# Starting byte of the moving rows, by stage: 0 (or 64) before, four remainders of 128 after

## The chip, the cores and the metric

One core of one Trainium2 chip runs the whole program. The metric is the device time of that core in microseconds; the time before is 2819.22 us, the median of two runs (2818.82 and 2819.62).

## What is computed

Two transformer-like blocks over 512 tokens of width 1024, all in float32. The reference, cut to its frame:

```
for i in range(2):                                   # first block
    h = h + 0.5 * swiglu(rms_norm(h, ffn1_norm[i]), w_in, w_out)
    h = h + mixer(rms_norm(h, mix_norm[i]))          # recurrent, then spatial gating
    h = h + 0.5 * swiglu(rms_norm(h, ffn2_norm[i]), w_in, w_out)
h = rms_norm(h, final_norm)
h = h + merged @ w_out                               # attention, S5 and HGRN2 branches
h = h + cross_attention(rmsnorm(h), rmsnorm(mem), ...)
h = h + swiglu_2(rmsnorm(h), w_gate_up, w_down)
```

There are five feed-forward parts (numbered i = 0 to 4 below): up to 2 x 2816 columns, SiLU, and down to 1024.

## The kernel before

**Products in three passes.** Each float32 operand is split into a high and a low part (type F32R): ACT writes the high part (w_hi, xg_hi, h_hi), POOL or DVE the difference (w_lo, xg_lo, h_lo). A product of two tiles is three matmuls into the same bank: high by high (L460), high weights by low rows (L461), low weights by high rows (L462), in `three_passes`. Weights are the stationary operand, 128 x 128; the moving operand is one row of 512 tokens per partition, `hi` or `lo`.

**Stages.** x (x_res) holds the residual, [128, 8, 512]. At each norm, number q, xg_hi and xg_lo are written from x by the gains. The norms are q = 0, 2, 3, 5, 9 (the five feed-forward parts), 1 (recurrent mixer), 4 (spatial gating mixer), FINAL = 6 (input of the second block and its branches) and 8 (cross-attention). All nine use the same two buffers in turn.

**The up projection** (`pe_ffn`) runs its first units and its last body as plain three-pass products with 512-token rows: 192 such matmuls in each of parts 1 to 4, 288 in part 0. The rest goes in steps of seven block products of 12 matmuls each, with rows of 256 tokens (L716, L717, L718): three of them read halves of xg, four read xsum, a tile of four sums of blocks of x, high and low, [4, 2, 4, 256]. One step is 36 matmuls on xg and 48 on xsum; there are 16 steps in part 0 and 18 in each other part.

**The down projection** reads h_hi and h_lo, [22, 512] each, 528 matmuls in each part. h_raw lies where h_lo will be written.

**The mixers.** q = 1 has 16 units of 24 matmuls on xg rows, q = 4 has 8, q = 8 has 8, and q = FINAL has 48. In the value projections of q = 4 and FINAL and one branch (L547 to L549 and L2030 to L2032, 384 matmuls) xg is the stationary operand and the weights move.

**Addresses.** `place` gives every tile a fixed byte offset within the partition. x_res begins at a multiple of 2048 and the tiles up to `work` have sizes that are multiples of 2048, so xg_hi, xg_lo, w_hi, w_lo, h_hi and h_lo all begin at a multiple of 128, and so does each of their rows. mem_hi, mem_lo (the memory of the cross-attention), yh, sgy, y0, y1, merged and o begin at multiples of 1024 above `work`, too. One exception: xsum begins at `work + 64`, so each of its rows of 1024 bytes begins 64 bytes past a multiple of 128.

**Order.** SP loads weights into a ring of four units, ACT and POOL split them, PE multiplies, DVE and ACT take the banks. The order on every engine is written out by hand; semaphores alone hold it together.

Of the kernel before, what the change touches and what calls it, by code (L numbers as in the profile page):

```python
# [91 lines left out]
def build(nc, io):  # L92
# [51 lines left out]


    LINE = 2048
    cursor = [-(-nc.sbuf_base // 128) * 128]

    def place(name, shape, dt=F32, at=None):
# [12 lines left out]
    eps = place("eps", [P, 1])  # L162
    cursor[0] = -(-cursor[0] // LINE) * LINE
    x = place("x_res", [P, KD, T])
    xg_hi = place("xg_hi", [P, KD, T], F32R)
    xg_lo = place("xg_lo", [P, KD, T], F32R)
    w_stage = place("w_stage", [P, RING, UNIT])
    w_hi = place("w_hi", [P, RING, UNIT], F32R)
    w_lo = place("w_lo", [P, RING, UNIT], F32R)
# [6 lines left out]
    aux = cursor[0]  # L176
    cursor[0] += 8192
    work = cursor[0]
    h_hi = place("h_hi", [P, KF, T], F32R)
    h_lo = place("h_lo", [P, KF, T], F32R)  # L180
    par = place("par", [P, NPAR])
    ones = place("ones", [P, P])
    ident = place("ident", [P, P])
# [2 lines left out]
    KB = 1024  # L186


    h_raw = place("h_raw", [P, KF, T], at=work + KF * T * 4)
    xsum = place("xsum", [P, 4, 2, 4, HALF], F32R, at=work + 64)  # L190
    s1_w = place("s1_w", [P, 2, T], F32R, at=work + 33 * KB)
    s2_w = place("s2_w", [P, 2, T], F32R, at=work + 37 * KB)
    u_add0 = place("u_add0", [P, T], at=work + 41 * KB)
# [370 lines left out]
        return KD * (q - (q > FINAL))  # L564

    def act_norm_tile(act, q, gain, m, buf):
        act.activation(tile(xg_hi, m), tile(x, m), ACT.Copy, scale=col(*gain(m))).then_inc(xg_hi_ready, 1)
        act_norm_square(act, q, m, buf)

    def act_norm_square(act, q, m, buf):  # L570
# [3 lines left out]

    def dve_norm_tile(dve, q, gain, m, buf):
        dve.wait_ge(xg_hi_ready, m + (split_count(q) + 1))
        dve.scalar_tensor_tensor(tile(xg_lo, m), tile(x, m), col(*gain(m)), f32(tile(xg_hi, m)),
                                 ALU.mult, ALU.subtract).then_inc(xg_lo_ready, 1)
        dve_norm_add(dve, q, m, buf)
# [128 lines left out]

    def pe_ffn(pe, i, q):
        U, L = layers[f"up{i}"], layers[f"down{i}"]  # L710

        def product(out, w, v):
            (wh, wl), (xh, xl) = w, v
# [76 lines left out]
        each_body(pe, L.bodies, down)  # L790

    def pool_up(pool, U, i):

        def plain(b, u):
            if U.base == 0 and b == 0 and u == 1:
                pool.wait_ge(xg_lo_ready, KD)
            split_lo_unit(pool, U, b, u)

        def row(b, p, row):
            r = 2 * p + row  # L800
            cs = slice(row * T, 2 * T)
# [12 lines left out]

        def s3_low(n):
            pool.wait_ge(wsum_hi_ready, after_wsum_hi(i, "S3", n))
            pool.tensor_tensor(s3_w[:, 1], s3_f[:], f32(s3_w[:, 0]), ALU.subtract).then_inc(pool_lo_ready, 1)

        def scale_gate(j):

            pool.wait_ge(silu_done, j + (KF * i + 1))
            pool.tensor_tensor(gbuf[:], gbuf[:], rstd[:], ALU.mult).then_inc(silu_scaled, 1)

        def step(b, p, gate=True):
            n, b1, p1 = pair_at(b, p), b + p, 1 - p
            row(b1, p1, 0)
            if gate:
                scale_gate(n + 1)
            s3(n + 1, p1)
            row(b1, p1, 1)  # L830
            s3_low(n + 1)

        at = PLAIN_FIRST[i]
        n0 = pair_at(at, 0)
        for u in range(3):
            plain(0, u)
        if i == 0:
            plain(0, 3)
            for u in range(3):
                plain(1, u)  # L840
        pool.wait_ge(xsum_done, XSUMS * (i + 1))
        plain(at - 1, 3)
        s3(n0, 0)
        x_low(0)
        row(at, 0, 0)
        x_low(3)
        row(at, 0, 1)
        x_low(2)
        s3_low(n0)
        x_low(1)  # L850
        step(at, 0, gate=False)
        step(at, 1)
        with pool.Fori(at + 1, LAST - 1) as b:
            step(b, 0)
            step(b, 1)
        step(LAST - 1, 0)
        plain(LAST, 0)
        scale_gate(KF - 4)
        plain(LAST, 1)
        plain(LAST, 2)  # L860
        scale_gate(KF - 3)
        plain(LAST, 3)
# [5 lines left out]

    def act_x_high(act, i, t):
        act.wait_ge(xsum_done, XSUMS * i + XSUM_COUNT[t])  # L870
        act.activation(xsum[:, t, 0], xsum_f[:, 1 + t], ACT.Copy).then_inc(wsum_hi_ready, 1)

    def act_ffn_entry(act, i, gain):

# [24 lines left out]

    def act_ffn(act, i, gain):  # L900
        U, L = layers[f"up{i}"], layers[f"down{i}"]

        def row1(b, p):
            split_hi(act, U, b, 2 * p)
# [101 lines left out]

    def dve_ffn(dve, i, gain=None):
        U = layers[f"up{i}"]

        def wsum(name, b, n, p):  # L1010
            w11, w12, w22 = w_stage[:, 2 * p, 0:T], w_stage[:, 2 * p, T:2 * T], w_stage[:, 2 * p + 1, T:2 * T]
# [208 lines left out]
    def pe_rec(pe, q):  # L1220
# [12 lines left out]
        for s in range(2 * KD):  # L1233
            u = s % KD
            if s == KD + 4:
                pe.wait_ge(gates_sig, 2 * KD)
            project_unit(pe, R if s < KD else Y, u // 4, u % 4, xg_hi, xg_lo,
                         (xg_lo_ready, split_count(q)) if s == 0 else None, out=y_bank(u) if s >= KD else None)
            if s == 0:
                pe_norm_sum(pe, q)  # L1240
            if 0 <= s - GATES_AT < KD:
                gates(s - GATES_AT)
# [126 lines left out]
    def pe_sgu(pe, q):  # L1369
# [5 lines left out]
        def norms_read(pe):  # L1375
            pe.wait_ge(std_ready, q + 1)
            pe.wait_ge(col_std, 1)
        pe_project_tokens(pe, V, xg_hi, xg_lo, norm=norms, ready=(xg_lo_ready, split_count(q)), between=norms_read)

        def mix(h):  # L1380

# [6 lines left out]
                               start=True, stop=True)  # L1388
            mm.then_inc(mixed, 1)
        for u in range(KD):  # L1390
            project_unit(pe, U, u // 4, u % 4, xg_hi, xg_lo, free=V.rbase + u + 1 if u < 4 else None)
            if u == 2:
                pe.wait_ge(ws_ready, 1)
                mix(0)
                mix(1)
            if u >= 2:
                mix(u)
# [95 lines left out]
    def dve_final(dve, L):  # L1493
# [8 lines left out]
        def body(b):  # L1502
            for mm in range(4):
                m = b * 4 + mm
                dve.wait_ge(unit_used, b * L.per + (L.base + (mm + 1) * 3))
                dve.scalar_tensor_tensor(tile(x, m), bank[mm][:], 0.5, tile(x, m), ALU.mult, ALU.add).then_inc(taken, 1)
                dve.wait_ge(xg_hi_ready, m + (KD * FINAL + 1))
                dve.scalar_tensor_tensor(tile(xg_lo, m), tile(x, m), gain12[:, bass.ds(m, 1)], f32(tile(xg_hi, m)),
                                         ALU.mult, ALU.subtract).then_inc(xg_lo_ready, 1)
                dve.wait_ge(ss_added, m * 2 + added)  # L1510
# [10 lines left out]
    def act_final(act, L):  # L1521
        act.wait_ge(final_gain, 1)

        def result(b, i):
            if i % 3 == 2:
                m = b * 4 + i // 3
                act.wait_ge(taken, m + (L.rbase + 1))
                act.activation(tile(xg_hi, m), tile(x, m), ACT.Copy, scale=gain12[:, bass.ds(m, 1)]).then_inc(xg_hi_ready, 1)
                act.wait_ge(ss_added, m * 2 + ((KD + 1) * FINAL + 2))
                act.activation(sq[:, 0, :], tile(x, m), ACT.Square).then_inc(sq_ready, 1)  # L1530
                act.activation(sq[:, 1, :], tile(x, m), ACT.Square, scale=col("final_norm", m)).then_inc(sq_ready, 1)
# [82 lines left out]
    def pe_fox_unit(pe, kind, i):  # L1614
# [7 lines left out]
            pe.wait_ge(taken, L.rbase + i - 1)  # L1622
        else:
            pe.wait_ge(taken, L.rbase + i)
        for k in range(KD):
            mm = three_passes(pe, unit_bank(kind, i)[:], r, k, xg_hi[:, k, :], xg_lo[:, k, :], k == 0, k == KD - 1)
        mm.then_inc(unit_used, 1)
# [25 lines left out]

    def pe_mix(pe):
        V = layers["fox_v"]
        pe_project_tokens(pe, V, xg_hi, xg_lo, norm=pe_final_sums, ready=(xg_lo_ready, split_count(FINAL + 1)), norm_after=2)

        def pack_squares(p):
# [348 lines left out]
    def pe_s5(pe):  # L2007
        QFG, V, M = layers["hg_qfg"], layers["hg_v"], layers["merge01"]

        def first_half(u):  # L2010
# [7 lines left out]
                pe.wait_ge(w_lo_ready, V.base + u - 12 + 1)  # L2018
            half(u, 0)

        def half(u, part):

            if 12 <= u < 16:
# [258 lines left out]

    def pe_merge_gate(pe, b, p, i, ks=range(KD)):
        L, u, r, _ = triple(b, p)
        if ks[0] == 0:
            pe.wait_ge(w_lo_ready, L.base + u + i + 1)
            pe.wait_ge(taken, L.rbase + r + i + 1 - RING)
# [305 lines left out]

    def pe_cross(pe):
        Q, O = layers["xq"], layers["xo"]

        def q_half(u, part):
            if part == 0:
# [656 lines left out]
    def _(act):  # L3255
# [4 lines left out]
        split_hi(act, order[0], 0, 0)  # L3260
        for m in range(KD):
            act.wait_ge(x_in[m // 2], 32)
            act.activation(xg_hi[:, m, :], x[:, m, :], ACT.Copy, scale=col("ffn1_norm", m)).then_inc(xg_hi_ready, 1)
        split_hi(act, order[0], 0, 1)
        for m in range(KD):
            act_norm_square(act, 0, m, m % 2)
# [30 lines left out]
    def _(dve):  # L3297
        dve.wait_ge(par_in, 16)
        dve.memset(ss[:], 0.0).then_inc(ss_added, 1)
        for m in range(KD):  # L3300
            dve.wait_ge(x_in[m // 2], 32)
            dve.wait_ge(xg_hi_ready, m + 1)
            dve.scalar_tensor_tensor(xg_lo[:, m, :], x[:, m, :], col("ffn1_norm", m), f32(xg_hi[:, m, :]),
                                     ALU.mult, ALU.subtract).then_inc(xg_lo_ready, 1)
        for m in range(KD):
            dve_norm_add(dve, 0, m, m % 2)
# [170 lines left out]
```

## Time and profile before

| | |
|---|---|
| median of two runs | 2819.22 us |
| the profiled execution, its span | 2817.5 us |
| PE busy | 2790.9 us (99%), 16386 matmuls |
| weight loads (PEld) | 2391.3 us (85%) |
| DVE | 1657.6 us (59%) |
| POOL | 1571.1 us (56%) |
| ACT | 1346.4 us (48%) |
| matmuls on the chain that ended last | 94% of the span |
| DMA | 267.91 MB, mean 95 GB/s |

The time of a matmul in the profile includes its way through the array, so consecutive matmuls overlap in the listing: a 512-token matmul shows 389 ns but the next starts 0.22 or 0.23 us after it. What a matmul costs in a dense stretch is the distance from its start to the next start, and that is read from the timeline, or from a window divided by the matmuls that the program has in it.

### The profile page before, as it was taken

To read this page: it belongs to the slowest core of one execution; us is meant where nothing else is said; L and a number is where in the kernel's file an instruction comes from. 1 tells how busy PE (TensorE), PEld (TensorE's weight loads), DVE (VectorE), ACT (ScalarE), POOL (GpSimd) and SP (SyncE) were. 2 spreads that over 40 slices of the span, in tenths; PEclk is the share of its full clock that TensorE was granted. 3 is DMA by queue.
4 is the path that set the end of the run, shared out by engine and by line. 5 is a ranking of instruction groups with operands and counts; after the bars stand their busy time and mean duration, and the time that the engine had idled before them with its cause. 6 is when DMAs were issued, how large, how long until landed. Compare 5 with 4: busy or idle time off the path is not lost.

```text
span 2817.5 us, 45558 instructions
## 1 busy us (share of the span) xinstructions
PE 2790.9 (99%) x16386; PEld 2391.3 (85%) x16386; DVE 1657.6 (59%) x2703; ACT 1346.4 (48%) x2076; POOL 1571.1 (56%) x872
## 2 busy tenths in 40 slices
PE   8999999999999999999999999999999999999999
PEld 6998877899889998888999886665688888799987
DVE  6777147677616774135777416579788464477730
ACT  5554257555425554243555334557444444455531
POOL 6775445677547774444777443158633373367743
PEclk9999999999999999999999999999999999999999
DMA  3234322232332233332223332112222342123332
GB/s 136 105 104 115 103 82 82 91 104 104 111 99 90 104 109 105 100 106 89 91 104 120 101 94 77 53 53 66 71 89 70 103 149 75 53 103 107 109 98 77
DMA packets 80685, 267.91 MB, mean 95 GB/s; under 512 B 11168, under 2 KB 13216, under 8 KB 80560
## 3 DMA queue, kind: packets, MB, share of 16 engines
q1 hardware_dynamic: 77904, 262.01, 28.4%
q10 hardware_dynamic: 2656, 4.26, 0.5%
q8 instruction: 74, 1.21, 0.2%
q14 instruction: 51, 0.42, 0.0%
HBM read 263.09 MB, written 2.10 MB: 94 GB/s over the span
## 4 chain that ended last, share of the span: by engine, by line
PE 94%; DVE 3%; ACT 1%; issue 1%; DMA 0%; POOL 0%; ACTq 0%; SPq 0%; DVEq 0%
PE bank L460 17%; PE bank L462 17%; PE bank L461 17%; PE bank L716 10%; PE bank L718 10%; PE bank L717 10%; PE bank L547 1%; PE bank L548 1%; PE bank L549 1%; PE bank L1635 1%; PE bank L2047 1%; PE bank L2915 1%; PE bank L2647 0%; PE bank L2056 0%; PE bank L2627 0%
## 5 line engine op out<-in xcount | busy, mean ns | idle before, releaser
L448 POOL TENSOR_TENSOR w_lo<-w_stage,w_hi 128x1024 fp32r<-128x1024 f32 (+1 forms) x228 | 535.2, 2353 | 714.0 <-ACT w_hi L424 713.5
L424 ACT ACTIVATE w_hi<-w_stage 128x1024 fp32r<-128x1024 f32 (+1 forms) x412 | 421.0, 1027 | 367.2 <-PE bank L462 303.5
L803 POOL TENSOR_TENSOR w_lo<-w_stage,w_hi 128x1024 fp32r<-128x1024 f32 (+1 forms) x176 | 327.3, 1859 | 202.1 <-ACT w_hi L424 202.1
L460 PE MATMUL bank<-xg_hi,w_hi 128*128 128x512 f32 x976 | 396.2, 406 | 5.0 <-DVE h_raw L1063 3.8
L461 PE MATMUL bank<-xg_lo,w_hi 128*128 128x512 f32 x976 | 381.2, 391 | 0.0
L462 PE MATMUL bank<-xg_hi,w_lo 128*128 128x512 f32 x976 | 381.2, 391 | 0.0
L455 POOL TENSOR_TENSOR w_lo<-w_stage,w_hi 128x1024 fp32r<-128x1024 f32 (+1 forms) x96 | 234.9, 2453 | 261.7 <-ACT w_hi L424 217.3
L460 PE MATMUL bank<-h_hi,w_hi 128*128 128x512 f32 x880 | 342.3, 389 | 0.0
L461 PE MATMUL bank<-h_lo,w_hi 128*128 128x512 f32 x880 | 342.3, 389 | 0.0
L462 PE MATMUL bank<-h_hi,w_lo 128*128 128x512 f32 x880 | 342.3, 389 | 0.0
L718 PE MATMUL bank<-xg_hi,w_lo 128*128 128x256 f32 x1056 | 299.2, 283 | 0.0
L716 PE MATMUL bank<-xg_hi,w_hi 128*128 128x256 f32 x1056 | 298.9, 283 | 0.0
L717 PE MATMUL bank<-xg_lo,w_hi 128*128 128x256 f32 x1056 | 298.8, 283 | 0.0
L716 PE MATMUL bank<-xsum,s_w 128*128 128x256 f32 x1056 | 296.1, 280 | 0.0
L718 PE MATMUL bank<-xsum,s_w 128*128 128x256 f32 x1056 | 294.6, 279 | 0.0
L717 PE MATMUL bank<-xsum,s_w 128*128 128x256 f32 x1056 | 294.6, 279 | 0.0
L1136 DVE SCALAR_TENSOR_TENSOR x_res<-bank,x_res 128x512 f32 x64 | 44.0, 687 | 400.9 <-PE bank L462 400.9
L460 PEld LDWEIGHTS bank<-xg_hi,w_hi 128*128 128x128 f32 x976 | 183.6, 188 | 72.5 <-issue 34.5
L1028 DVE TENSOR_TENSOR s_w<-bank,s_w 128x512 fp32r<-128x512 f32 x176 | 121.7, 691 | 190.4 <-ACT s_w L933 190.4
L461 PEld LDWEIGHTS bank<-xg_lo,w_hi 128*128 128x128 f32 x976 | 183.9, 188 | 40.5 <-issue 4.8
L462 PEld LDWEIGHTS bank<-xg_hi,w_lo 128*128 128x128 f32 x976 | 183.6, 188 | 39.7
L716 PEld LDWEIGHTS bank<-xg_hi,w_hi 128*128 128x128 f32 x1056 | 202.4, 192 | 0.2
(530 smaller groups left out, 6599.0 us busy)
## 6 DMA issues: line engine op xcount, KB each, us to landing
w_stage<-w_up SPq DMA_DIRECT2D x220, 512.0 KB, 4.2
w_stage<-w_down SPq DMA_DIRECT2D x80, 512.0 KB, 3.5
w_stage<-merge SPq DMA_DIRECT2D x36, 512.0 KB, 3.4
w_stage<-w_down SPq DMA_DIRECT2D x40, 384.0 KB, 3.2
w_stage<-hg_qfg SPq DMA_DIRECT2D x12, 512.0 KB, 3.4
w_stage<-rec_r SPq DMA_DIRECT2D x8, 512.0 KB, 3.5
w_stage<-rec_y SPq DMA_DIRECT2D x8, 512.0 KB, 3.4
w_stage<-rec_out SPq DMA_DIRECT2D x8, 512.0 KB, 3.4
```

What stands on the lines that cost most here:

```text
L424: act.activation(w_hi[:, r, 0:w], w_stage[:, r, 0:w], ACT.Copy).then_inc(w_hi_ready, 1)
L448: pool.tensor_tensor(w_lo[:, r, 0:w], w_stage[:, r, 0:w], f32(w_hi[:, r, 0:w]), ALU.subtract).then_inc(w_lo_ready, 1)
L455: pool.tensor_tensor(w_lo[:, r, 0:w], w_stage[:, r, 0:w], f32(w_hi[:, r, 0:w]), ALU.subtract).then_inc(w_lo_ready, 1)
L460: pe.matmul(out, w_hi[:, r, c], hi, start=start, stop=False)
L461: pe.matmul(out, w_hi[:, r, c], lo, start=False, stop=False)
L462: return pe.matmul(out, w_lo[:, r, c], hi, start=False, stop=stop)
L716: pe.matmul(out, wh[:, c], xh[:, k, :], start=k == 0, stop=False)
L717: pe.matmul(out, wh[:, c], xl[:, k, :], start=False, stop=False)
L718: mm = pe.matmul(out, wl[:, c], xh[:, k, :], start=False, stop=k == 3)
L803: pool.tensor_tensor(w_lo[:, r, cs], w_stage[:, r, cs], f32(w_hi[:, r, cs]), ALU.subtract).then_inc(w_lo_ready, 1)
L1028: dve.tensor_tensor(lo, src[:], f32(hi), ALU.subtract).then_inc(wsum_lo_ready, 1)
L1136: dve.scalar_tensor_tensor(tile(x, m), bank[mm % 4][:], scale, tile(x, m), ALU.mult, ALU.add).then_inc(taken, 1)
```

## The change

Nothing is computed differently and nothing is reordered: every engine has the same instructions in the same order, with other addresses. The buffer pair of xg is replaced by nine views into a region that is larger by 2 x 2048 bytes, one pair for each norm; h_hi, h_lo, h_raw and xsum get one view per feed-forward part, in a work region that is also larger by 2 x 2048 bytes. Each view begins at a remainder of 0, 32, 64 or 96 bytes by 128, and since rows are 1024 or 2048 bytes long each row of it does. The DMA scratch that the program reserves at the front of the on-chip memory is set to 1024 bytes, which frees the space.

```
+    XG_REMAINDER = {0: (64, 64), 1: (0, 96), 2: (32, 32), 3: (96, 96), 4: (64, 0), 5: (0, 64), FINAL: (64, 64), 8: (96, 32),
+                    9: (0, 32)}
+    XSUM_REMAINDER = (32, 96, 0, 64, 64)
+    H_REMAINDER = ((64, 64), (32, 32), (96, 96), (0, 64), (32, 96))
...
-    xg_hi = place("xg_hi", [P, KD, T], F32R)
-    xg_lo = place("xg_lo", [P, KD, T], F32R)
+    XG_BASE = cursor[0]
+    xg_of = {q: (place(f"xg_hi{q}", [P, KD, T], F32R, at=XG_BASE + high),
+                 place(f"xg_lo{q}", [P, KD, T], F32R, at=XG_BASE + KD * T * 4 + LINE + low)) for q, (high, low) in XG_REMAINDER.items()}
+    cursor[0] += 2 * (KD * T * 4 + LINE)
...
-    h_hi = place("h_hi", [P, KF, T], F32R)
-    h_lo = place("h_lo", [P, KF, T], F32R)
+    h_of = [(place(f"h_hi{i}", [P, KF, T], F32R, at=work + high),
+             place(f"h_lo{i}", [P, KF, T], F32R, at=work + KF * T * 4 + LINE + low)) for i, (high, low) in enumerate(H_REMAINDER)]
+    cursor[0] += 2 * (KF * T * 4 + LINE)
...
-    h_raw = place("h_raw", [P, KF, T], at=work + KF * T * 4)
-    xsum = place("xsum", [P, 4, 2, 4, HALF], F32R, at=work + 64)
+    h_raw_of = [place(f"h_raw{i}", [P, KF, T], at=work + KF * T * 4 + LINE + low) for i, (_, low) in enumerate(H_REMAINDER)]
+    xsum_of = [place(f"xsum{i}", [P, 4, 2, 4, HALF], F32R, at=work + off) for i, off in enumerate(XSUM_REMAINDER)]
...
     def pe_ffn(pe, i, q):
         U, L = layers[f"up{i}"], layers[f"down{i}"]
+        xg_hi, xg_lo = xg_of[q]
+        h_hi, h_lo = h_of[i]
+        xsum = xsum_of[i]
...
-    nc = bacc.Bacc("TRN2", target_bir_lowering=False, num_devices=1)
+    nc = bacc.Bacc("TRN2", target_bir_lowering=False, num_devices=1, dynamic_dma_scratch_size=1024)
```

The other lines of the diff replace the names xg_hi, xg_lo, h_hi, h_lo, h_raw and xsum by the view of the stage at hand.

By what the moving rows of a matmul have (high, low), the matmuls that the change touches are:

| remainders | 512-token rows | 256-token rows |
|---|---|---|
| 64 and 64 (part 0: xg, h; FINAL: xg) | 288 + 528 + 1152 = 1968 | 576 |
| 32 and 32, 96 and 96, 32 and 96, 96 and 32 (parts 1, 2: xg, h; part 4: h; q = 8: xg) | 720 + 720 + 528 + 192 = 2160 | 1296 |
| 0 with 64, 64 with 0 (part 3: xg, h; q = 4: xg) | 720 + 192 = 912 | 648 |
| 0 with 32, 0 with 96 (part 4: xg; q = 1: xg) | 192 + 384 = 576 | 648 |
| xsum 64 to 32 or 96 (parts 0, 1) | | 768 + 864 = 1632 |
| xsum 64 to 0 (part 2) | | 864 |
| xsum unchanged at 64 (parts 3, 4) | | 1728 |

## Rows read from the trace of the kernel before

**Rows 1.** The page: span, busy times, granted clock, and the chain's shares.
```profile
span 2817.5 us, 45558 instructions
...
PE 2790.9 (99%) x16386; PEld 2391.3 (85%) x16386; DVE 1657.6 (59%) x2703; ACT 1346.4 (48%) x2076; POOL 1571.1 (56%) x872
...
PEclk9999999999999999999999999999999999999999
...
PE 94%; DVE 3%; ACT 1%; issue 1%; DMA 0%; POOL 0%; ACTq 0%; SPq 0%; DVEq 0%
```

**Rows 2.** Waits of PE, longest first: whom it waited for, total, times, longest.
```profile
PE bank L486 <- ACT xg_hi L3263: 8.2, 1, 8.2
PE bank L460 <- DVE h_raw L1063: 3.8, 1, 3.8
```

**Rows 3.** One down projection, then up: window, its length, PE busy (records), clock, DMA.
```profile
1080.20:1199.90 119.70, 119.70 (x530) 1.00 0.33 99
1362.10:1541.70 179.60, 179.60 (x1513) 1.00 0.32 112
```

**Rows 4.** Timeline, PE, 512-token rows: start, time, operation (first and last of 47).
```profile
868.19 0.39 PE L461 MATMUL bank<-xg_lo,w_hi 128*128 128x512 f32 x1
...
878.85 0.28 PE L716 MATMUL bank<-xg_hi,w_hi 128*128 128x256 f32 x1
```

**Rows 5.** Timeline, PE: 256-token rows of xg, first and last of 31.
```profile
947.79 0.28 PE L718 MATMUL bank<-xg_hi,w_lo 128*128 128x256 f32 x1
...
951.51 0.28 PE L716 MATMUL bank<-xsum,s_w 128*128 128x256 f32 x1
```

**Rows 6.** Timeline, PE: 256-token rows of mem, eleven starts.
```profile
2254.80 0.28 PE L462 MATMUL bank<-mem_hi,w_lo 128*128 128x256 f32 x1
...
2256.00 0.28 PE L460 MATMUL bank<-mem_hi,w_hi 128*128 128x256 f32 x1
```

**Rows 7.** Timeline, PE: the 48 xsum matmuls of a step in steady running.
```profile
941.53 0.28 PE L716 MATMUL bank<-xsum,s_w 128*128 128x256 f32 x1
941.65 0.28 PE L717 MATMUL bank<-xsum,s_w 128*128 128x256 f32 x1
...
947.19 0.29 PE L716 MATMUL bank<-xg_hi,w_hi 128*128 128x256 f32 x1
947.32 0.28 PE L717 MATMUL bank<-xg_lo,w_hi 128*128 128x256 f32 x1
947.43 0.29 PE L718 MATMUL bank<-xg_hi,w_lo 128*128 128x256 f32 x1
```

**Rows 8.** Timeline, PE: the xsum matmuls behind a hesitation at 891.78.
```profile
891.58 0.28 PE L718 MATMUL bank<-xg_hi,w_lo 128*128 128x256 f32 x1
891.78 0.35 PE L716 MATMUL bank<-xsum,s_w 128*128 128x256 f32 x1
891.97 0.28 PE L717 MATMUL bank<-xsum,s_w 128*128 128x256 f32 x1
...
897.29 0.28 PE L716 MATMUL bank<-xg_hi,w_hi 128*128 128x256 f32 x1
```

**Rows 9.** Timeline, PE: 512-token rows after a hesitation, in the recurrent mixer.
```profile
475.81 0.40 PE L461 MATMUL bank<-yh_lo,w_hi 128*128 128x512 f32 x1
476.05 0.39 PE L462 MATMUL bank<-yh_hi,w_lo 128*128 128x512 f32 x1
...
477.19 0.39 PE L461 MATMUL bank<-yh_lo,w_hi 128*128 128x512 f32 x1
```

**Rows 10.** Groups of weight loads, 940 to 960 us: busy, mean ns.
```profile
L716 PEld LDWEIGHTS bank<-xg_hi,w_hi 128*128 128x128 f32 x25 | 4.8, 192 | 0.0
L716 PEld LDWEIGHTS bank<-xsum,s_w 128*128 128x128 f32 x24 | 4.5, 188 | 0.0
```

**Rows 11.** POOL's waits in the up projections, and the page's DMA queues.
```profile
POOL w_lo L803 <- ACT w_hi L424: 202.1, 79, 4.8
...
q1 hardware_dynamic: 77904, 262.01, 28.4%
q10 hardware_dynamic: 2656, 4.26, 0.5%
```

More of the change, by code:

```diff
@@ L566, in act_norm_tile @@
     def act_norm_tile(act, q, gain, m, buf):
-        act.activation(tile(xg_hi, m), tile(x, m), ACT.Copy, scale=col(*gain(m))).then_inc(xg_hi_ready, 1)
+        act.activation(tile(xg_of[q][0], m), tile(x, m), ACT.Copy, scale=col(*gain(m))).then_inc(xg_hi_ready, 1)
         act_norm_square(act, q, m, buf)
@@ L710, in pe_ffn @@
         U, L = layers[f"up{i}"], layers[f"down{i}"]
+        xg_hi, xg_lo = xg_of[q]
+        h_hi, h_lo = h_of[i]
+        xsum = xsum_of[i]
         def product(out, w, v):
@@ L792, in pool_up @@
     def pool_up(pool, U, i):
+        xsum = xsum_of[i]
         def plain(b, u):
@@ L870, in act_x_high @@
         act.wait_ge(xsum_done, XSUMS * i + XSUM_COUNT[t])
-        act.activation(xsum[:, t, 0], xsum_f[:, 1 + t], ACT.Copy).then_inc(wsum_hi_ready, 1)
+        act.activation(xsum_of[i][:, t, 0], xsum_f[:, 1 + t], ACT.Copy).then_inc(wsum_hi_ready, 1)
     def act_ffn_entry(act, i, gain):
@@ L901, in act_ffn @@
         U, L = layers[f"up{i}"], layers[f"down{i}"]
+        h_hi, h_raw = h_of[i][0], h_raw_of[i]
         def row1(b, p):
@@ L1008, in dve_ffn @@
         U = layers[f"up{i}"]
+        (h_hi, h_lo), h_raw = h_of[i], h_raw_of[i]
         def wsum(name, b, n, p):
@@ L1236, in pe_rec @@
                 pe.wait_ge(gates_sig, 2 * KD)
-            project_unit(pe, R if s < KD else Y, u // 4, u % 4, xg_hi, xg_lo,
+            project_unit(pe, R if s < KD else Y, u // 4, u % 4, *xg_of[q],
                          (xg_lo_ready, split_count(q)) if s == 0 else None, out=y_bank(u) if s >= KD else None)
@@ L1377, in norms_read @@
             pe.wait_ge(col_std, 1)
-        pe_project_tokens(pe, V, xg_hi, xg_lo, norm=norms, ready=(xg_lo_ready, split_count(q)), between=norms_read)
+        pe_project_tokens(pe, V, *xg_of[q], norm=norms, ready=(xg_lo_ready, split_count(q)), between=norms_read)
         def mix(h):
@@ L1390, in pe_sgu @@
         for u in range(KD):
-            project_unit(pe, U, u // 4, u % 4, xg_hi, xg_lo, free=V.rbase + u + 1 if u < 4 else None)
+            project_unit(pe, U, u // 4, u % 4, *xg_of[q], free=V.rbase + u + 1 if u < 4 else None)
             if u == 2:
@@ L1507, in body @@
                 dve.wait_ge(xg_hi_ready, m + (KD * FINAL + 1))
+                xg_hi, xg_lo = xg_of[FINAL]
                 dve.scalar_tensor_tensor(tile(xg_lo, m), tile(x, m), gain12[:, bass.ds(m, 1)], f32(tile(xg_hi, m)),
@@ L1527, in result @@
                 act.wait_ge(taken, m + (L.rbase + 1))
-                act.activation(tile(xg_hi, m), tile(x, m), ACT.Copy, scale=gain12[:, bass.ds(m, 1)]).then_inc(xg_hi_ready, 1)
+                act.activation(tile(xg_of[FINAL][0], m), tile(x, m), ACT.Copy, scale=gain12[:, bass.ds(m, 1)]).then_inc(xg_hi_ready, 1)
                 act.wait_ge(ss_added, m * 2 + ((KD + 1) * FINAL + 2))
@@ L1624, in pe_fox_unit @@
             pe.wait_ge(taken, L.rbase + i)
+        xg_hi, xg_lo = xg_of[FINAL]
         for k in range(KD):
@@ L1655, in pe_mix @@
         V = layers["fox_v"]
+        xg_hi, xg_lo = xg_of[FINAL]
         pe_project_tokens(pe, V, xg_hi, xg_lo, norm=pe_final_sums, ready=(xg_lo_ready, split_count(FINAL + 1)), norm_after=2)
@@ L2019, in first_half @@
             half(u, 0)
+        xg_hi, xg_lo = xg_of[FINAL]
         def half(u, part):
@@ L2284, in pe_merge_gate @@
         L, u, r, _ = triple(b, p)
+        xg_hi, xg_lo = xg_of[FINAL]
         if ks[0] == 0:
@@ L2595, in pe_cross @@
         Q, O = layers["xq"], layers["xo"]
+        xg_hi, xg_lo = xg_of[8]
         def q_half(u, part):
@@ L3262, in _ @@
             act.wait_ge(x_in[m // 2], 32)
-            act.activation(xg_hi[:, m, :], x[:, m, :], ACT.Copy, scale=col("ffn1_norm", m)).then_inc(xg_hi_ready, 1)
+            act.activation(xg_of[0][0][:, m, :], x[:, m, :], ACT.Copy, scale=col("ffn1_norm", m)).then_inc(xg_hi_ready, 1)
         split_hi(act, order[0], 0, 1)
@@ L3302, in _ @@
             dve.wait_ge(xg_hi_ready, m + 1)
-            dve.scalar_tensor_tensor(xg_lo[:, m, :], x[:, m, :], col("ffn1_norm", m), f32(xg_hi[:, m, :]),
+            dve.scalar_tensor_tensor(xg_of[0][1][:, m, :], x[:, m, :], col("ffn1_norm", m), f32(xg_of[0][0][:, m, :]),
                                      ALU.mult, ALU.subtract).then_inc(xg_lo_ready, 1)
```

## Prediction

> **What bounds the kernel now.** I read the page first. PE is busy for 2790.9 of 2817.5 us, its clock is at full rate in all 40 slices (the higher of its two levels, 2.4 GHz), and matmuls make 94% of the chain that ended last [rows 1]. Then the waits of PE: the longest is 8.2 us at the very start, the next 3.8 us, so there is no stall of any size to win [rows 2]. What is left is the rate of the stream of matmuls itself, and for that busy time says nothing; I go to the distance between starts.
>
> At 2.4 GHz and one column a cycle, a row of 512 tokens takes 213.3 ns and one of 256 takes 106.7 ns. The starts are further apart:
>
> - 512-token rows at remainder 0: a down projection has 528 matmuls in 119.7 us, 226.7 ns each [rows 3]; in the timeline 47 of them take 10.66 us, 226.8 ns each [rows 4]. That is 13.3 ns over the columns.
> - 256-token rows of xg at remainder 0: 31 take 3.72 us, 120.0 ns [rows 5]. Again 13.3 ns over.
> - 256-token rows of mem, also at remainder 0, but 1024 bytes apart as the rows of xsum are: ten take 1.20 us, 120.0 ns [rows 6].
> - 256-token rows of xsum at remainder 64: 48 take 5.66 us, 117.9 ns [rows 7], 11.2 ns over.
> - the same rows in the one step that follows a hesitation of PE: from 891.97 to 897.29 there are 47 matmuls in 5.32 us, 113.2 ns each [rows 8], 6.5 ns over.
>
> So every matmul pays a fixed 6.5 to 13.3 ns at its edge, whatever its length, and the sum over the span is large: 5616 + 3168 matmuls at 13.3 ns and 4224 at 11.2 are 164 us. The edge cost differs between remainder 0 and remainder 64, and at 64 it has two steady values, one of which is entered by a pause and left again at the next xg row. The rows of mem are what makes me put the difference to the remainder and not to the distance between rows or to the tile.
>
> **The change part by part.** No instruction is added, removed or moved; each term is (matmuls touched) x (change of distance). The counts are in the table of the change.
>
> *64 with 64: 1968 + 576 = 2544 matmuls.* The nearest rows are those of xsum. Between 120.0 and 117.9 the gain is 2.1 ns; between 120.0 and 113.2 it is 6.8. In these stages no row at 0 comes between to break the better rhythm, but I can't see how it is entered at 512 tokens, and in part 0 xsum, at 32, comes between. I take the middle, 4.45 ns: 2544 x 4.45 = 11.3 us gained (5.3 to 17.3).
>
> *32 and 96 with each other or themselves: 2160 + 1296 = 3456 matmuls.* No moving row of the trace has such a remainder. It could be as good as the best row seen (-6.8 ns), and a row that begins in mid-unit could cost the same again. For the far side the nearest row is that of 512-token matmuls which have just lost their rhythm: 475.81 to 477.19 is six in 1.38 us, 230 ns, 3.3 over the settled 226.7, and the first of them takes 0.24 us, up to 13 over [rows 9]; I put the far bound between, at +6.8. Halfway is nothing: 0 us, with -23.5 and +23.5 as bounds.
>
> *0 with 64 or 64 with 0: 912 + 648 = 1560 matmuls.* A third or two thirds of the rows are at 64, and the passes alternate. Alternation itself has a price in the trace: the entry from xg to xsum takes 0.12 us, and after the return to xg the starts are at 947.19, 947.32, 947.43, one longer and one shorter [rows 7]; it evens out. I take a third of 4.45: 1560 x 1.5 = 2.3 us gained (0 to 10.6).
>
> *0 with 32 or 96: 576 + 648 = 1224.* As the 32 and 96 case, a third of the rows: 0 us, bounds -2.8 and +2.8; and if mixed pairs behave as their worse member, +8.3.
>
> *xsum.* At 0 (864 matmuls) it should run as xg and mem do, 120.0 for 117.9: 1.8 us lost. At 32 and 96 (1632 matmuls) I take the same 120.0, as I took nothing against 0 for the others: 3.4 us lost, bounds 113.2 (7.7 gained) and 126.8 (14.5 lost). Unchanged at 64 (1728): 0, but up to 8.1 us gained if the better rhythm now holds.
>
> *xg as the stationary operand, 384 matmuls.* The weight loads beside xg rows at 0 take 192 ns and those beside xsum at 64 take 188 [rows 10]; they run beside the matmul before them, and PE waits for none. 0 us, with 384 x 6.8 = 2.6 us either way.
>
> *Other engines.* ACT, DVE and POOL write and read the same sizes at other starts. They have room: POOL in the up projections waits 202.1 us for ACT [rows 11], and PE waits for none of them [rows 2]. If one were slower by a tenth it would still be covered; without this cover each split of a unit would be on the path. A faster PE by 3 to 6% in a stage leaves the same room. The queues that carry data are hardware queues [rows 11], so the smaller scratch costs nothing.
>
> Sum: -11.3 + 0 - 2.3 + 0 + 1.8 + 3.4 = -8.4 us. The profiled execution would go from 2817.5 to 2809.1 us; the median of the runs lies 1.7 above the span, so I forecast **2811 us**.
>
> The Trainium skill, TensorE: Matmul & The Clock Gate, section "Back-to-back issue gap", gives a spacing of columns over 2.4 GHz plus about 2.5 ns. By that page rows of 512 would stand at 215.8 ns and rows of 256 at 109.2 ns, wherever they begin. The trace has 226.7 and 120.0 [rows 3, 5] and so disagrees: there is an excess in this stream that the page does not know.
>
> **The rivals.**
>
> *The remainder does nothing* (chance 0.17). The difference between xg and xsum would come from the tile's place or from what runs beside it. For it: within a tile at 64 the distance has two values without any change of address [rows 7, 8], so the remainder does not set it alone. Against it: mem at 0 behaves as xg [rows 5, 6]. Time: 2819 us, within 3. The Trainium skill, Advanced Engine Details and Errata, section "SBUF Cachelines", has lines of 16 bytes; by that page all four remainders begin on a line and nothing would change. No row here tells lines of 16 bytes from others.
>
> *Only the coincidence with the weights is dear* (chance 0.25). Weight rows begin at 0, and a load runs beside each matmul; it takes 192 ns beside rows at 0 and 188 beside rows at 64 [rows 10]. If any other start than 0 avoids the collision, then the 32 and 96 rows gain the same 4.45 ns, and mixed pairs half. 6000 x 4.45 = 26.7, 2784 x 2.2 = 6.1, less 1.8 for xsum at 0: 31 us faster, 2788 us. Against it: at 512 tokens the loads show 188 ns and yet 13.3 ns are lost. The Trainium skill, TensorE: Matmul & The Clock Gate, section "Step-by-step: what each phase is for", says that weights and moving rows come through two independent read ports; by that page this rival falls.
>
> *A row that begins within a unit of 64 bytes needs one fetch more* (chance 0.16, slower than before). The step between the edge costs seen, 13.3 and 6.5 ns, is the time of 16 columns, 64 bytes. Rows at 32 or 96 would cover one such unit more: 3456 x 6.8 = 23.5, a third of 1224 x 6.8 = 2.8, xsum at 32 and 96 at 126.8: 1632 x 8.9 = 14.5, xsum at 0: 1.8; less 11.3 and 2.3. That is +29 us, 2848 us. It decides the sign: break-even is where an off-unit row costs 1.5 ns more than a row at 0 (5496 such rows, counted as above, against the 8.4 us of the forecast).
>
> *The better rhythm takes over* (chance 0.07). All rows but those at 0 at 6.8 ns less, xsum at 113.2: 5616 + 3168 matmuls at 6.8 is 59.7, xsum 3360 x 4.7 = 15.8, less 1.8: about 74 us faster, 2745 us.
>
> *Off-unit rows lose far more than an edge* (chance 0.04): read at half rate, 3456 + 1632 matmuls would each take 100 ns or more on top, over 500 us. The trace shows no such row, hence the small chance is not zero.
>
> The forecast itself, only 64 helping and 32 and 96 being about as 0, has 0.31.
>
> **How the numbers follow.** The forecast alone spans 2800 to 2820. The range for 8 in 10 takes in the coincidence, nothing, and the extra fetch, and leaves out the last two and the tails: 2776 to 2850 us. Two per cent is about what a measurement of this kernel can tell from no change: 2762.8 and 2875.6 us. Faster by more than that needs most of the better rhythm: 0.07, and a little of the coincidence at its full 6.8 ns, 0.02. Slower by more needs the half-rate case or twice the extra fetch: 0.05. The rest, 0.86, is within.
>
> **What would show each step.** In the timeline: h of part 0 and xg of FINAL (64, 64) at 222 ns a matmul, the down projection of part 0 near 117.5 us instead of 119.7; parts 1 and 2 (32 and 96) at 119.7 still; xsum of part 2 at 120.0. The coincidence rival shows parts 1, 2 and 4 as short as part 0; the extra fetch shows them at 233 ns, 123 us; the rival of no effect leaves all at 119.7. I am wrong altogether if PE gets waits that it did not have, or if equal remainders give different distances in different parts without a pause between.

## The result and the profile after

The changed kernel takes 2842.74 us (median of two runs, 2842.48 and 2843.01) against 2819.22 us. The ratio is 1.0077 with an interval of 1.0053 to 1.0102: 23.5 us slower. The time is inside the range of the prediction and on the other side of its forecast, 2811.

The page of the kernel after, the rows that answer to [rows 1]:

```profile
span 2840.7 us, 45558 instructions
...
PE 2811.4 (99%) x16386; PEld 2387.6 (84%) x16386; DVE 1660.8 (58%) x2703; ACT 1346.0 (47%) x2076; POOL 1573.2 (55%) x872
...
PEclk9999999999999999999999999999999999999999
...
PE 94%; DVE 3%; ACT 1%; issue 1%; DMA 0%; POOL 0%; ACTq 0%; SPq 0%; DVEq 0%
```

The span is 23.2 us longer with the same instructions, the same clock and the same chain. The waits of PE, to hold against [rows 2]:

```profile
PE bank L493 <- ACT xg_hi L3284: 8.5, 1, 8.5
PE bank L467 <- DVE h_raw L1077: 6.5, 1, 6.5
```

They are 3.0 us longer together. Both lie in the first 42 us; in the traces of the other kernels below the second is between 2.7 and 4.3 us, so its 6.5 is at least in part a matter of the single execution. About 20 us went into the stream of matmuls. The five down projections of the kernel after, in windows that begin with their first matmul and end with the one behind their last, or, for the fifth, which has none behind it, with the start of its last (columns: window, its length, PE busy with records, clock, DMA):

```profile
244.70:365.60 120.90, 120.90 (x530) 1.00 0.33 98
740.20:863.40 123.20, 123.20 (x529) 1.00 0.31 96
1090.40:1213.60 123.20, 123.20 (x530) 1.00 0.32 96
1578.60:1701.10 122.50, 122.50 (x530) 1.00 0.30 88
2714.60:2837.00 122.40, 122.40 (x528) 1.00 0.28 86
```

Before, each of them took 119.7 us [rows 3], the fifth 119.5 to the start of its last matmul. From the start of the first matmul to the start of the last (527 distances, which is finer than a window read to 0.1 us) one distance is 228.9 ns for h at (64,64), 233.3 for (32,32) and for (96,96), 232.0 for (0,64) and 232.2 for (32,96), against 226.7. The five add up to 612.2 us against 598.3: 13.9 us of the 23.

The 256-token rows went the other way. Timeline of PE in the kernel after, the 36 matmuls on xg of a step in part 0, first and the one behind the last:

```profile
122.92 0.28 PE L727 MATMUL bank<-xg_hi,w_hi 128*128 128x256 f32 x1
...
127.16 0.28 PE L727 MATMUL bank<-xsum,s_w 128*128 128x256 f32 x1
```

4.24 us for 36, 117.8 ns each, where they had 120.0 [rows 5].

I summed the distances from start to start in both traces by stage and row length. The shares of the 23 us (a span of values goes over the stages, each with its own remainders):

| rows | before to after, ns a matmul | sum, us |
|---|---|---|
| h, 512 tokens | 226.7 to 228.9 ... 233.3 | +13.9 |
| xg, 512 tokens (waits in between included) | about 227 to 229 ... 233 | +10.3 |
| weights of 512 moving, xg stationary | 227 to 233 | +2.0 |
| xg, 256 tokens | 120.1 to 117.6 ... 120.0 | -5.5 |
| xsum, 256 tokens | 117.8 to 116.8 (32), 119.8 (96), 119.8 (0) | +2.0 |

The third line was not in my sum as a cost. Timeline of PE in the kernel after, 17 distances where the weights move and xg at (64,0) is loaded:

```profile
1226.02 0.40 PE L555 MATMUL bank<-w_hi,xg_lo 128*128 128x512 f32 x1
...
1229.99 0.39 PE L554 MATMUL bank<-w_hi,xg_hi 128*128 128x512 f32 x1
```

3.97 us for 17, 233.5 ns, though the moving rows begin at 0 as before.

The settled distances are not spread evenly. A product of two tiles is three matmuls, and three of them take 680.0 ns at 226.7, 686.7 at 228.9 and 700.0 at 233.3; kernels below have 693.3, at 231.1. That is a step of 6.67 ns each time. At 256 tokens three matmuls take 360.0 ns at 120.0, 353.3 at 117.8 and 340.0 at 113.3: one such step down from the first to the second, and two more to the third. Values between, as 232.0 and 232.2, are averages over longer patterns. The traces show the steps, not their cause.

### The profile page after: what moved, and what is told of

The parts are those of the page before. It is cut to its first block, busy times and chain, and to the rows that moved or that the text cites. A ratio compares the mean times of both kernels' runs of the same rounds, so it can differ in the third digit from the quotient of the medians.

```text
span 2840.7 us, 45558 instructions
## 1 busy us (share of the span) xinstructions
PE 2811.4 (99%) x16386; PEld 2387.6 (84%) x16386; DVE 1660.8 (58%) x2703; ACT 1346.0 (47%) x2076; POOL 1573.2 (55%) x872
## 4 chain that ended last, share of the span: by engine, by line
PE 94%; DVE 3%; ACT 1%; issue 1%; DMA 0%; POOL 0%; ACTq 0%; SPq 0%; DVEq 0%
PE bank L467 18%; PE bank L469 17%; PE bank L468 17%; PE bank L729 10%; PE bank L727 10%; PE bank L728 10%; PE bank L556 1%; PE bank L555 1%; PE bank L554 1%; PE bank L1651 1%; PE bank L2066 1%; PE bank L2936 1%; PE bank L2668 0%; PE bank L2075 0%; PE bank L2648 0%
## 5 line engine op out<-in xcount | busy, mean ns | idle before, releaser
L467 PEld LDWEIGHTS bank<-xg_hi,w_hi 128*128 128x128 f32 x976 | 183.7, 188 | 78.2 <-issue 37.2
L728 PEld LDWEIGHTS bank<-xsum,s_w 128*128 128x128 f32 x1056 | 199.6, 189 | 0.0
```

Of the source, the lines that this page charges most:

```text
L467: pe.matmul(out, w_hi[:, r, c], hi, start=start, stop=False)
L728: pe.matmul(out, wh[:, c], xl[:, k, :], start=False, stop=False)
```

## The experiments

All kernels are the changed one with other numbers in its three tables; in four of them the weight tiles are moved too. Distances are read from each kernel's own trace. Ratios are against the kernel before on the same chip.

**1. Layout or remainders, and whose.** Four kernels. The first has every remainder as before in the changed layout:

```
-    XG_REMAINDER = {0: (64, 64), 1: (0, 96), 2: (32, 32), 3: (96, 96), 4: (64, 0), 5: (0, 64), FINAL: (64, 64), 8: (96, 32),
-                    9: (0, 32)}
-    XSUM_REMAINDER = (32, 96, 0, 64, 64)
-    H_REMAINDER = ((64, 64), (32, 32), (96, 96), (0, 64), (32, 96))
+    XG_REMAINDER = {0: (0, 0), 1: (0, 0), 2: (0, 0), 3: (0, 0), 4: (0, 0), 5: (0, 0), FINAL: (0, 0), 8: (0, 0), 9: (0, 0)}
+    XSUM_REMAINDER = (64, 64, 64, 64, 64)
+    H_REMAINDER = ((0, 0), (0, 0), (0, 0), (0, 0), (0, 0))
```

> The changed kernel with every remainder as before: xg and h at 0, xsum at 64, in the changed layout (regions larger by 4 x 2048 bytes, w and work tiles moved, scratch 1024). The theory that the remainders cost the time: 2819 us, down projections 119.7 us each, as in the kernel before. The rival that the layout or the scratch costs it: about 2843 us.

Measured: 2819.27 us, ratio 0.9993 (0.9983 to 1.0003). Larger regions, moved weights and the smaller scratch cost nothing; the remainders are the cause. In its trace the five down projections stand at 226.7 ns again.

The second keeps only the H_REMAINDER of the change, the third only its XG_REMAINDER, the fourth only its XSUM_REMAINDER.

> Only h has the new remainders; xg at 0, xsum at 64. If each matmul pays by its own row's remainder, the five down projections keep the lengths of the changed kernel, 120.9, 123.2, 123.2, 122.5 and 122.4 us against 119.7, which is +13.9 us in sum: 2833 us. If the loss comes from what surrounds them (the rhythm brought in from the up projection, xg), they return towards 119.7 and the time is under 2825.

Measured: 2835.27 us, ratio 1.0047 (1.003 to 1.0064), 14.8 us over the kernel before in the same comparison (2820.48). Its down projections, in order:

```profile
246.50:367.40 120.90, 120.90 (x530) 1.00 0.33 98
740.00:863.20 123.20, 123.20 (x529) 1.00 0.31 96
...
1574.50:1697.00 122.50, 122.50 (x529) 1.00 0.29 88
2712.50:2834.90 122.40, 122.40 (x529) 1.00 0.29 86
```

These are the lengths of the changed kernel to 0.1 us, whatever the up projection ahead of them has, and so is the third, left out here, at 123.3 us. For 512-token rows the cost is local to the rows.

> Only xg has the new remainders; h at 0, xsum at 64. Summing the distances between starts over xg rows in the traces of before and after gives +7 us: 2826 us, the 512-token rows slower (227 to 229 to 233 ns), the 256-token rows faster (120 to about 118). If rows influence each other, xsum at 64 beside xg at 64 (part 0) takes up the better rhythm, 113.3 ns, and the time is lower by up to 3.5 us.

Measured: 2823.01 us, ratio 1.0007 (0.9997 to 1.0016). The 512-token rows were slower by as much as in the changed kernel. Less was lost than expected because part 1, with xg at (32,32) and xsum at 64, ran its xsum rows at 114.4 ns instead of 117.9, 3 us. Part 0, with both at 64, did not: 117.6 ns. The guess of the expectation on where the better rhythm would appear was wrong.

> Only xsum has the new remainders (32, 96, 0, 64, 64); xg and h at 0. By the distances in the two traces the xsum rows give -0.8, +1.6, +1.8, -0.2, -0.3 us: +2 us, 2821 us. If the distance of xsum is set by its own remainder alone, part 2 (now at 0, as xg) stands at 120.0 ns and parts 3 and 4 at 117.9 exactly as before.

Measured: 2823.64 us, ratio 1.0011 (1.0002 to 1.0021). xsum at 96 and at 0 stands at 120.1 and 120.0 ns, 1.8 and 2.0 us; at 32, with xg at 0, it stands at 117.9, not at the 116.8 that it has beside xg at 64. So for 256-token rows the neighbours count. The three parts of the change make 14.8 + 2.5 + 3.2 = 20.5 us of the 23.5. The intervals of these ratios are 5 to 10 us wide, so the times alone would not show what is missing; the traces do: part 1 gained 3.0 us on xsum only while xsum stayed at 64.

**2. The unit.** The weights stay at 0 and h gets pairs that the change did not have.

```
+    H_REMAINDER = ((64, 0), (0, 32), (32, 0), (128, 128), (64, 32))
```

> xg at 0, xsum at 64; h of the five parts at (64,0), (0,32), (32,0), (128,128), (64,32). The period is 128 if part 3 stands at 226.7 ns, as (0,0). If a row pays by its own remainder alone, a pair is the weighted mean of its two values (0: 226.7, 64: 229.0, 32: 233.3; high rows count twice): 228.2, 228.9, 231.1, 226.7, 230.4 ns. If the change from one remainder to the other also costs, as (0,64) with 232.0 in the changed kernel suggests, the mixed pairs are well above that, up to 233.

Measured, ns a matmul: 233.3, 231.7, 233.3, 233.3, 231.1. (128,128) was meant as a repeat of (0,0):

```profile
1574.40:1697.60 123.20, 123.20 (x530) 1.00 0.29 88
```

123.2 us instead of 119.7. "Remainder by 128" is the wrong description. And a pair need not be the mean of its members: (64,0) costs more than either (64,64) or (0,0).

**3. Against what.** The weights w_hi and w_lo are moved, to 64 and then to 32 above a multiple of 128.

```
-    w_hi = place("w_hi", [P, RING, UNIT], F32R)
-    w_lo = place("w_lo", [P, RING, UNIT], F32R)
+    w_hi = place("w_hi", [P, RING, UNIT], F32R, at=cursor[0] + 64)
+    w_lo = place("w_lo", [P, RING, UNIT], F32R, at=cursor[0] + RING * UNIT * 4 + 128 + 64)
+    cursor[0] += 2 * RING * UNIT * 4 + LINE
+    H_REMAINDER = ((0, 0), (64, 64), (32, 32), (96, 96), (64, 0))
```

> The weights w_hi and w_lo begin at 64 in all stages; h of the parts at (0,0), (64,64), (32,32), (96,96), (64,0). If only the moving row's own remainder counts, the first four down projections stand at 226.7, 229.0, 233.3, 233.3 ns a matmul as with the weights at 0. If the distance between the remainders of weights and rows counts, 0 and 64 change places: 229.0, 226.7, 233.3, 233.3. If the weights add their own share, as the stationary xg at 64 did in the changed kernel (233.3 ns), all are dearer, the first at 233.3.

> The weights begin at 32; h at (0,0), (64,64), (32,32), (96,96), (32,96). Only the row's own remainder: 226.7, 229.0, 233.3, 233.3, 232.2 ns. The distance between both: (32,32) stands at 226.7, (96,96) at 229.0, (0,0) and (64,64) at 233.3. Own share of the weights: every part is above its value with the weights at 0, by up to 6.7 ns.

Measured, one execution each, weights at 64: 231.8, 231.1, 233.3, 233.3, 231.1 ns; weights at 32: 231.1, 233.3, 231.1, 233.3, 231.1. All three readings fail as they were put. But the weights' place does count: with not one byte of h moved, the first part went from 119.7 to 122.4 us. What spoils these two runs is that w_lo lies another 128 bytes further on than w_hi, which I had thought to be no shift at all.

The whole time of the kernel with the weights at 64, 2835.05 us, hides its best part. Timeline of PE, the 36 matmuls on xg of a step in part 2 and the row behind them:

```profile
947.17 0.29 PE L727 MATMUL bank<-xg_hi,w_hi 128*128 128x256 f32 x1
...
951.29 0.28 PE L727 MATMUL bank<-xsum,s_w 128*128 128x256 f32 x1
```

4.12 us for 36 is 114.4 ns, where the kernel before has 120.0, and all five parts have it. Summed over the trace the 256-token rows of xg gained 18.0 us and those of xsum 2.6, with no moving row of the up projections shifted by a byte. The down projections and the other 512-token rows took it back. So at 256 tokens the place of the weights counts as well. The five placements of h beside these weights all cost 231.1 ns or more; no other was tried.

So once more, cleanly, with starts counted from a multiple of 2048. First with the weights at 0 and h at larger steps:

```
+    H_REMAINDER = ((256, 256), (512, 512), (1024, 1024), (192, 192), (0, 128))
```

> Weights at 0, xg at 0, xsum at 64; h of the five parts at (256,256), (512,512), (1024,1024), (192,192), (0,128). The pair (128,128) stood at 233.3 ns, not at the 226.7 of (0,0), so 128 bytes is not the period of the effect. If the period is 256, the first three parts stand at 226.7 ns and (192,192) at 229.0 (as 64) or 233.3 (as 32 and 96). If it is 512, 1024 or 2048, the first, the first two or all three are above 226.7. If any start but a multiple of 2048 is dear, all five stand at 229 to 233.

```profile
243.90:363.60 119.70, 119.70 (x529) 1.00 0.33 99
736.20:855.90 119.70, 119.70 (x530) 1.00 0.32 99
1079.90:1199.60 119.70, 119.70 (x529) 1.00 0.33 99
1563.40:1686.60 123.20, 123.20 (x529) 1.00 0.29 88
2697.60:2818.20 120.60, 120.60 (x528) 1.00 0.29 87
```

256, 512 and 1024 bytes are as good as 0; 192 costs the full 233.3 ns. The fifth, (0,128), stands at 228.9 ns, which for once is the mean of its members, with the high rows counted twice. Of the periods that these starts can tell apart it is 256 bytes.

Then with both weight tiles at 64, and with both at 128:

```
-    w_hi = place("w_hi", [P, RING, UNIT], F32R)
-    w_lo = place("w_lo", [P, RING, UNIT], F32R)
+    w_hi = place("w_hi", [P, RING, UNIT], F32R, at=cursor[0] + 64)
+    w_lo = place("w_lo", [P, RING, UNIT], F32R, at=cursor[0] + RING * UNIT * 4 + LINE + 64)
+    cursor[0] += 2 * (RING * UNIT * 4 + LINE)
+    H_REMAINDER = ((0, 0), (64, 64), (128, 128), (256, 256), (32, 32))
```

> Both w_hi and w_lo exactly 64 bytes above a multiple of 2048 (in the run with the weights at 64, w_lo lay at 192 by 256, which counts if 128 is not the period); h at (0,0), (64,64), (128,128), (256,256), (32,32). If the distance between rows and weights sets the cost, (64,64) stands at 226.7 ns and (0,0) above. If absolute starts set it, (64,64) stands at 229.0 or above, and no part reaches 226.7.

```profile
243.60:366.80 123.20, 123.20 (x530) 1.00 0.32 96
739.80:859.50 119.70, 119.70 (x530) 1.00 0.33 99
1081.60:1202.50 120.90, 120.90 (x530) 1.00 0.32 98
1567.10:1690.30 123.20, 123.20 (x530) 1.00 0.29 88
2708.70:2831.60 122.90, 122.90 (x528) 1.00 0.28 86
```

Rows at 64 are now the cheapest, 119.7 us, and rows at 0 are dear, 123.2.

> Weights exactly 128 above a multiple of 2048; h at (0,0), (128,128), (64,64), (256,256), (192,192). Distance between rows and weights: (128,128) at 226.7 ns, (192,192) at 229.0 as (64,64) with the weights at 0, (0,0) and (256,256) above. Absolute starts: (128,128) at 233.3 again.

```profile
242.40:365.60 123.20, 123.20 (x530) 1.00 0.32 96
737.30:857.00 119.70, 119.70 (x529) 1.00 0.32 99
1078.40:1201.60 123.20, 123.20 (x529) 1.00 0.31 96
1565.90:1689.00 123.10, 123.10 (x529) 1.00 0.29 88
2705.50:2826.10 120.60, 120.60 (x528) 1.00 0.29 87
```

With d = (start of the moving row - start of the weights) by 256 bytes, every down projection of the kernels that have w_hi and w_lo at the same place, and h_hi and h_lo too, falls into one table:

| d | weights at 0 | weights at 64 | weights at 128 |
|---|---|---|---|
| 0 | 226.7 (h at 0, 256, 512, 1024) | 226.7 (64) | 226.7 (128) |
| 64 | 228.9 (64) | 228.9 (128) | 228.9 (192) |
| 32, 96, 224 | 233.3 (32; 96) | 233.3 (32) | |
| 128 | 233.3 (128) | | 233.3 (0; 256) |
| 192 | 233.3 (192) | 233.3 (0; 256) | 233.3 (64) |

The stationary xg fits in as well. With both parts of xg at 64 and the moving weights at 0 (the changed kernel, FINAL) d is 192, and 72 matmuls stood at 233.4 ns; with xg at 0 and the moving weights at 64 d is 64, and the same 72 stood at 229.0. The (64,0) above, 233.5, is a mixed pair.

The other 512-token rows agree less exactly. With the weights at 128 and rows at 0 the distances in the mixers and up projections run from about 232 to 233.3 ns, and xg at 160 with the weights at 0 stood at 234.2. Only multiples of 32 bytes were tried. What it is in the chip that pays by this distance no run shows.

**4. The 256-token rows.** Tables of xg and xsum with h and the mixers at 0. A scan by part:

```
+    XG_REMAINDER = {0: (32, 32), 1: (0, 0), 2: (32, 0), 3: (32, 64), 4: (0, 0), 5: (64, 32), FINAL: (0, 0), 8: (0, 0), 9: (32, 96)}
+    XSUM_REMAINDER = (64, 64, 64, 64, 64)
```

> h at 0, mixers at 0, xsum at 64 in all parts; xg of the five parts at (32,32), (32,0), (32,64), (64,32), (32,96). With xg at (32,32) beside xsum at 64 the run of xg alone had 114.4 ns on xsum and 117.1 on xg in part 1. If that goes by the remainders, part 0 shows the same 114.4 and 117.1, and a matmul's distance is set by its neighbours' remainders as well as its own; if it was an accident of that part's entry, part 0 stays at 117.9. Time between 2812 and 2822 us.

Measured: 2812.6 us in its one timed run (before: 2819.98). Part 0 stayed at 117.6 ns on xsum although (32,32) with 64 had given part 1 114.4: the same starts, two rhythms. Part 1, now at (32,0), had 113.8; the others 117.8. This is close to the sign by which the prediction was to be wrong altogether, equal remainders with different distances in different parts, though here across two kernels.

The pair (32,0) in all five parts:

> h and mixers at 0, xsum at 64, xg of all five parts at (32,0). Part 1 had 113.8 ns on xsum, 118.0 on xg of 256 and 231.1 on xg of 512 with it, 4.2 us less than before. If the remainders give this, five parts give 21 us: 2798 us. If it was part 1's own entry, the other parts have 117.9 on xsum and the time is 2808 to 2813 us.

Measured: 2799.91 us, ratio 0.9925 (0.9908 to 0.9941): 0.75% faster than the kernel before, the best of all. The better rhythm holds in every part, at 113.8 to 114.1 ns over all steps, and is worth 16.7 us by the distances; the 256-token rows of xg gained 6.9, its 512-token rows lost about 4. Timeline of PE, the 48 xsum matmuls of a step in part 2 and the row behind them:

```profile
952.35 0.28 PE L726 MATMUL bank<-xsum,s_w 128*128 128x256 f32 x1
...
957.79 0.28 PE L726 MATMUL bank<-xg_hi,w_hi 128*128 128x256 f32 x1
```

5.44 us for 48 is 113.3 ns; the same 48 took 5.66 before [rows 7].

Then the guess that d = 192 is best at this length, since rows of mem at 0 beside weights at 64 ran so. Timeline of PE in the kernel with both weight tiles at 64, 20 distances:

```profile
2268.02 0.28 PE L468 MATMUL bank<-mem_lo,w_hi 128*128 128x256 f32 x1
...
2270.29 0.30 PE L467 MATMUL bank<-mem_hi,w_hi 128*128 128x256 f32 x1
```

2.27 us for 20 is 113.5 ns. Against the guess stood, in the same kernel, that the 256-token rows of xg, also at d = 192, had 117.8.

> Weights, h and mixers at 0 by 256; xg of the feed-forward parts and xsum at 192. With the weights at 64 and rows at 0 (a distance of 192 by 256) the undisturbed 256-token rows stood at 113.5 ns. If the distance alone sets it, all 256-token rows stand at 113.3: xg 648 x 6.7 = 4.3 us and xsum 864 x 4.6 = 4.0 us gained in a part, less 192 x 6.6 = 1.3 us for its 512-token rows (233.3, as every row at 192): 7 us a part, 35 us in all, 2785 us. If absolute starts matter for 256-token rows, it is above 2800 us.

Measured: 2817.17 us, ratio 0.9992 (0.9983 to 1.0001). Same distance, other rhythm, in all parts. Its 48 xsum matmuls:

```profile
950.39 0.28 PE L726 MATMUL bank<-xsum,s_w 128*128 128x256 f32 x1
...
956.04 0.28 PE L726 MATMUL bank<-xg_hi,w_hi 128*128 128x256 f32 x1
```

5.65 us, 117.7 ns. The distance from the weights alone does not set a 256-token row. Two scans by part went after what else does:

> As before, with xg / xsum of the five parts at 192/64, 192/128, 224/224, 160/160, 128/192 by 256. If each row goes by its own distance to the weights, xg stands at 113.3 in parts 0 and 1, xsum at 113.3 in part 4, and xsum at 117.9 in part 0. If a row's neighbours count, xg in part 0 is above 113.3. The starts 160 and 224 are off 64, and if a 256-token row needs more there, parts 2 and 3 stand at 118 to 120.

> Weights, h and mixers at 0; xg (high, low) / xsum of the five parts: (32,0)/192, (192,0)/64, (0,192)/64, (64,0)/192, (32,0)/128. In the run with xg at (32,0) and xsum at 64 all five parts had xsum at 113.8 to 114.1 ns. If the odd start of xg brings PE into the better rhythm, parts 0 and 4 have it with xsum at 192 and 128 too; if the pair (32,0) with 64 is a single case, they stand at 117.8 or above. If any high-low pair that differs does it, parts 1 to 3 have it as well.

Measured, xg (high, low) / xsum: distance of xg and of xsum in ns, over all steps of the part:

| xg / xsum | xg | xsum |
|---|---|---|
| (0,0) / 64, before | 120.1 | 117.9 |
| (192,192) / 64 | 117.7 | 117.8 |
| (192,192) / 128 | 114.5 | 118.9 |
| (224,224) / 224 | 118.3 | 118.3 |
| (160,160) / 160 | 118.7 | 118.7 |
| (128,128) / 192 | 118.8 | 113.6 |
| (32,0) / 192 | 117.8 | 113.3 |
| (192,0) / 64 | 118.4 | 117.8 |
| (0,192) / 64 | 117.8 | 114.2 |
| (64,0) / 192 | 118.7 | 117.8 |
| (32,0) / 128 | 117.9 | 118.7 |

The one timed run of each was 2815.29 and 2811.28 us. Unequal pairs do not bring the better rhythm by themselves, (192,0) and (64,0) lack it; (32,0) brings it with 64 and 192 and not with 128. The scans have one execution of each pair. The values between (114.2, 116.8) are mixtures or patterns of several distances, not a third rhythm that I could name. Which starts lead into which rhythm stays open.

## Why the prediction was wrong, point by point

**What bounds the kernel** held: PE's stream of matmuls, full clock, no other wait of weight, and an excess over the columns in each matmul. The formula of columns over 2.4 GHz plus 2.5 ns, which the prediction takes from the Trainium skill, TensorE: Matmul & The Clock Gate, section "Back-to-back issue gap", is given there for a matmul by itself; for a stream with weight loads the same section has about 131 ns at 512 columns. The trace has 226.7 and agrees with neither.

**The step that failed** is the one from the 256-token rows of xsum to the 512-token rows: "So every matmul pays a fixed 6.5 to 13.3 ns at its edge, whatever its length". At remainder 0 both lengths pay 13.3 ns, which hid that at other starts they do not. At 64 a 256-token row pays 11.2 and a 512-token row 15.6. I had the sign for 576 matmuls and put it on 1968 of the other length as well. The term of 64 with 64 was -11.3 us and came out at about +3: h of part 0 at +1.2, the 512-token rows of xg at +3.3 with the waits among them (settled at 228.9 ns in part 0), and only the 576 distances on xg of 256 in part 0's steps gained, 1.5 us.

**32 and 96** were put halfway between bounds of equal size, at 0. At 512 tokens they stand at the far bound, 233.3 ns, +6.7, near the +6.8 that I had taken from a stream that was finding its rhythm again [rows 9]. At 256 tokens they stand at 118.1 (32) and 120.0 (96), 2.0 and 0.1 gained. This is the largest share of the 23 us: the three down projections with such starts alone are 3.5 + 3.5 + 2.9 = 9.9 us, and the whole term came out at about +11 us, where the sum had nothing. The bound held it; that the middle of the bounds was taken had no row behind it.

**0 with 64** was to gain 2.3 us and lost about 3, 2.8 of it in h of part 3. The note there, that alternation has a price, was right; I then let it count for nothing. (64,0) at 233.3 beside (64,64) at 228.9 shows how large it is.

**xsum** had the right sign and was put too high: +5.2 forecast, +2.0 measured. 96 and 0 stand at 119.8 to 120.1 as said; 32, put at a loss of 1.6, gained 0.8, and the rows left at 64 gained 0.5.

**The stationary xg**, taken at 0, cost 2.0 us. PE waits for no weight load, as I wrote, but the start of what is loaded shifts the distance that the moving rows pay by.

**Other engines, layout and scratch** at 0: shown by the kernel with the old remainders, 0.9993.

**The rivals.** The one that came nearest is the extra fetch, 2848 us at a chance of 0.16: it had rows at 32 and 96 at +6.8 and down projections of 123 us, and they took 123.2. Its reason does not hold: by units of 64 bytes, starts of 128 and 192 would have been as good as 64, and both cost 233.3; and 64 lost where it was to gain. That its time, 2848, came near 2843 is in part luck: its loss of 14.5 us on xsum and its gain of 11.3 at 64, neither of which came, nearly cancel. The coincidence rival had the right pair of things, rows against weights, with the wrong sign: equal starts are the cheapest for 512-token rows, not the dearest. The Trainium skill, TensorE: Matmul & The Clock Gate, section "Step-by-step: what each phase is for", has weights and moving rows on two independent read ports, so that a weight load takes no read bandwidth from the matmul that runs. The table by d does not bear out that the two leave each other alone: moving the weights alone by 64 bytes adds 6.7 ns to each matmul of an unmoved row. The runs do not show what it is that the two share.

The observation that should have warned me stood in my own list: within one tile the distance had two values [rows 7, 8]. I used it as the width of a bound. It says that a remainder is not the variable, and that a value read from one stream is not to be carried to another.

## What to carry to other kernels

When a dense stream of F32R matmuls of 512 columns bounds a kernel, let moving rows and weights begin at the same place by 256 bytes; the other distances tried cost 2.2 to 6.7 ns of 227 in the down projections, up to 3% of a stage. For 256 columns these runs give single placements that were better, by as much as 18 us here, and no rule. Measure each row length by itself, by the distance from start to start over some tens of matmuls, and don't carry an edge cost from one length to another. A table by stage, such as this change has, tests many starts in one run, but then the whole time says little: read it by stage.

## What the runs showed of the hardware that I had not expected

- The spacing of 512-column matmuls goes by the start of the moving row less that of the weights, with a period of 256 bytes: 226.7 ns at 0, 228.9 at 64, 233.3 at 32, 96, 128, 192 and 224 in the down projections.
- Settled distances come in steps: three matmuls take 680.0, 686.7, 693.3 or 700.0 ns at 512 columns and 340.0, 353.3 or 360.0 at 256, multiples of one step of 6.67 ns apart. Mixed patterns lie between.
- At 256 columns the same addresses allow two rhythms, 113.3 and 117.9 ns, the better one behind a hesitation [rows 7, 8]; and (32,32) with 64 had 114.4 in one part and 117.6 in another. Rows at a distance of 192 stood at 117.7 in one kernel and at 113.5 in another. What ran before a row counts, and the weights' place too; the rule stays open.
- With w_hi at 64 and w_lo at 192 by 256 bytes, unmoved 256-token rows of xg went from 120.0 to 114.4 ns a matmul in every part.
- A pair of high and low rows with different starts need not be the mean of its members: (64,0) took 233.3 ns, (64,64) 228.9 and (0,0) 226.7.
